# A state space scan of 62 steps, divided by groups between VectorE and GpSimd

## The reference, cut to what matters

```
state[c + 1] = a8 * state[c] + s[c + 1]        (complex, a8 = a to the power 8)
```

## Time and profile before

| | us |
|---|---|
| median of 3 runs | 3091.88 (3086.79 to 3098.38) |
| the profiled execution, its own time | 3087.09 |
| its span | 3084.8 |
| TensorE busy | 2834.6 (92%) |
| VectorE busy | 1872.8 (61%) |
| ScalarE busy | 1415.3 (46%) |
| GpSimd busy | 261.6 (8%) |

### The profile page before, as it was taken

How to read it: one execution, slowest core, us unless ns; L and a number is a source line. 1 busy time by engine, 2 the same in 40 slices (tenths; PEclk the granted TensorE clock), 3 DMA queues, 4 the chain that set the end, 5 groups by cost and what they waited for, 6 DMA issues and landing times.

```text
span 3084.8 us, 35846 instructions
## 1 busy us (share of the span) xinstructions
PE 2834.6 (92%) x12864; PEld 2221.4 (72%) x12864; DVE 1872.8 (61%) x2184; ACT 1415.3 (46%) x1806; POOL 261.6 (8%) x267
## 2 busy tenths in 40 slices
PE   7999999995999999999996469999989989899998
PEld 2547888874777777777775358888877767788887
DVE  3435654454889899898988684544333785354432
ACT  2323333323777777777775423333223347433321
POOL 1100100061001001010111000000011100000000
PEclk9999999995999999999998779999999999899999
DMA  6920722313898999999896612222221110022221
GB/s 237 334 85 30 284 111 96 125 55 150 342 372 350 380 357 368 367 358 375 349 376 223 57 67 82 96 96 96 96 91 69 55 55 28 28 96 96 96 96 69
DMA packets 90801, 546.93 MB, mean 177 GB/s; under 512 B 9232, under 2 KB 18848, under 8 KB 32384
## 3 DMA queue, kind: packets, MB, share of 16 engines
q1 hardware_dynamic: 79584, 485.65, 42.2%
q0 software_dynamic: 10816, 59.58, 5.5%
q10 hardware_dynamic: 288, 0.15, 0.0%
HBM read 516.51 MB, written 41.42 MB: 181 GB/s over the span
## 4 chain that ended last, share of the span: by engine, by line
PE 74%; DVE 14%; issue 6%; ACT 4%; DMA 1%; POOL 1%; DVEq 0%; ACTq 0%; SPq 0%; POOLq 0%; PEldq 0%
PE bank L400 41%; PE bank L338 6%; PE bank L1284 6%; PE bank L1288 5%; PE bank L1287 5%; DVE expert_low L2345 3%; ACT expert_high L1744 1%; PE bank L1268 1%; PE bank L1535 1%; DVE expert_x_low L2430 1%; DVE arena L2474 1%; PE bank L1469 1%; DVE arena L2561 1%; DVE arena L2560 1%; PE bank L1392 1%
## 5 line engine op out<-in xcount | busy, mean ns | idle before, releaser
L2345 DVE TENSOR_TENSOR expert_low<-arena,expert_high 128x2048 fp32r<-128x2048 f32 x291 | 690.2, 2403 | 89.5 <-ACT expert_high L1744 71.9
L1744 ACT ACTIVATE expert_high<-arena 128x1024 fp32r<-128x1024 f32 x582 | 599.3, 1059 | 203.4 <-PE bank L1284 120.4
L803 DVE TENSOR_TENSOR weight_parts<-ring_pages,weight_parts 128x1024 fp32r<-128x1024 f32 x185 | 227.0, 1227 | 458.3 <-ACT weight_parts L795 457.9
L795 ACT ACTIVATE weight_parts<-ring_pages 128x1024 fp32r<-128x1024 f32 x185 | 195.9, 1060 | 450.6 <-PE bank L400 407.1
L400 PE MATMUL bank<-high_b,weight_parts 128*128 128x512 f32 x1168 | 372.6, 401 | 13.0 <-DVE low_p L2583 7.4
L400 PE MATMUL bank<-low_b,weight_parts 128*128 128x512 f32 x1056 | 353.9, 389 | 0.0
L1284 PE MATMUL bank<-expert_high,expert_x_low 128*128 128x512 f32 x768 | 305.3, 398 | 23.5 <-DVE expert_low L2345 21.9
L1288 PE MATMUL bank<-expert_low,expert_x_high 128*128 128x512 f32 x768 | 300.4, 391 | 0.0
L1287 PE MATMUL bank<-expert_high,expert_x_high 128*128 128x512 f32 x768 | 300.1, 391 | 0.0
L400 PEld LDWEIGHTS bank<-high_b,weight_parts 128*128 128x128 f32 x1168 | 219.4, 190 | 75.6 <-issue 25.0
L400 PEld LDWEIGHTS bank<-low_b,weight_parts 128*128 128x128 f32 x1056 | 198.2, 188 | 41.6 <-issue 0.5
(11 more groups left out here) (479 smaller groups left out, 4407.8 us busy)
## 6 DMA issues: line engine op xcount, KB each, us to landing
arena<-in_we_stream SPq DMA_DIRECT2D x294, 1024.0 KB, 6.6
ring_pages<-in_wb_stream SPq DMA_DIRECT2D x93, 1024.0 KB, 4.8
ring_pages<-in_wa_stream SPq DMA_DIRECT2D x49, 1024.0 KB, 4.8
arena<-in_mod POOLq DMA_DIRECT2D x16, 1024.0 KB
xbuf<-arena POOLq DMA_DIRECT2D x25, 512.0 KB, 15.9
arena<-xbuf SPq DMA_DIRECT2D x17, 512.0 KB, 7.3
ybuf<-arena SPq DMA_DIRECT2D x16, 512.0 KB, 2.6
arena<-kd SPq DMA_DIRECT2D x8, 512.0 KB, 21.2
```

The source lines that it names most:

```text
L795: nc.scalar.activation(high, src, ACT.Copy).then_inc(weights_high, 1)
L803: nc.vector.tensor_tensor(low, src, high.bitcast(F32), ALU.subtract).then_inc(weights_split, 1)
L1744: nc.scalar.activation(ehigh[c % HIGH_E][:, at], ring_e[c % RING_E][:, at], ACT.Copy) \
L2345: nc.vector.tensor_tensor(elow[c % RING_E][:], ring_e[c % RING_E], ehigh[c % HIGH_E][:].bitcast(F32), ALU.subtract).then_inc(weights_split ...
```

## The change

VectorE keeps groups 0 to 43 and GpSimd gets groups 44 to 63, so that a VectorE instruction covers 128 x 88 elements and a GpSimd one 128 x 40. GpSimd's 62 steps have the same form as VectorE's. TensorE waits for a signal of both.

```diff
+SCAN_DVE = 44
...
@@ GpSimd's stream, behind the DMAs of kd @@
+            pool.wait_ge(S["b_s_copied"], KT)
+            pool.wait_ge(S["b_upper_copied"], 3 * KT)
+            rest = slice(SCAN_DVE, S5G)
+            for c in range(1, S5C - 1):
+                steps[0] += 2
+                nc.gpsimd.tensor_tensor(scaled[:, 0, :, rest], xs[:, c, :, rest], ab8[:, 0, :, rest], ALU.mult) \
+                    .then_inc(pool_step, 1)
+                nc.gpsimd.tensor_tensor(scaled[:, 1, :, rest], xs[:, c, ::-1, rest], ab8[:, 1, :, rest], ALU.mult) \
+                    .then_inc(pool_step, 1)
+                pool.wait_ge(pool_step, steps[0])
+                link(nc.gpsimd.tensor_tensor(xs[:, c + 1, :, rest], xs[:, c + 1, :, rest], scaled[:, 0, :, rest], ALU.add))
+                link(nc.gpsimd.tensor_tensor(xs[:, c + 1, :, rest], xs[:, c + 1, :, rest], scaled[:, 1, :, rest], ALU.add))
+            pool.sem_inc(S["b_scanned"], 1)
@@ TensorE's stream @@
-            pe.wait_ge(S["b_scanned"], 1)
+            pe.wait_ge(S["b_scanned"], 2)
@@ VectorE's stream @@
-            ts = scaled
+            first = slice(0, SCAN_DVE)
+            ts = scaled[:, :, :, first]
             for c in range(1, S5C - 1):
-                part(nc.vector.tensor_tensor(ts[:, 0], xs[:, c, :, :], ab8[:, 0], ALU.mult))
-                part(nc.vector.tensor_tensor(ts[:, 1], xs[:, c, ::-1, :], ab8[:, 1], ALU.mult))
+                part(nc.vector.tensor_tensor(ts[:, 0], xs[:, c, :, first], ab8[:, 0, :, first], ALU.mult))
+                part(nc.vector.tensor_tensor(ts[:, 1], xs[:, c, ::-1, first], ab8[:, 1, :, first], ALU.mult))
                 dve.wait_ge(dve_step, steps[0])
-                link(nc.vector.tensor_tensor(xs[:, c + 1], xs[:, c + 1], ts[:, 0], ALU.add))
-                link(nc.vector.tensor_tensor(xs[:, c + 1], xs[:, c + 1], ts[:, 1], ALU.add))
+                link(nc.vector.tensor_tensor(xs[:, c + 1, :, first], xs[:, c + 1, :, first], ts[:, 0], ALU.add))
+                link(nc.vector.tensor_tensor(xs[:, c + 1, :, first], xs[:, c + 1, :, first], ts[:, 1], ALU.add))
             dve.sem_inc(S["b_scanned"], 1)
```

## The result

| | before | after |
|---|---|---|
| median of 20 runs each, us | 3091.05 (3082.48 to 3103.69) | 3099.39 (3088.12 to 3102.23) |
| span of the profiled execution, us | 3084.8 | 3097.3 |
| GpSimd busy, us | 261.6 | 325.6 |
| VectorE busy, us | 1872.8 | 1878.8 |

The ratio of the times is 1.0018, with a 95% interval of 1.001 to 1.0027: slower by 5.6 us (3.1 to 8.3). The ratio isn't the quotient of the medians in the table, which are 8.3 us apart, at the upper end of that interval; the means are 6.3 us apart. This text goes by the ratio. The effect is less than 0.5%, and it is clear of zero with twenty runs of each, though the executions of one kernel lie up to 21 us apart. The forecast had the sign, and 12.5 us.

What follows compares the result with a forecast made beforehand. The prediction took VectorE's scan, with TensorE waiting behind it, as the bound here. GpSimd's own pace (7.5 us) plus waits between the engines (5 us) gave 3091.9 + 12.5 = 3104.4 us, range 3088 to 3128.

Steps and rivals of the forecast that it cites:

- The bound: VectorE's scan of 62 steps, 73.1 us, keeps TensorE waiting; each microsecond of its end counts one for the whole.
- VectorE's share: VectorE's scan instructions at 88 elements take 251 ns, a step 1.01 us, 62 steps 62.8 us instead of 73.1.
- GpSimd's share: GpSimd's undisturbed scan of 20 groups: 0.266 us an instruction, 1.30 us a step, 80.9 us, ending 7.5 us later than before.
- The price of one meeting: In the scan, each engine keeps the other out for its own instruction's duration less 0.14 us.
- The meetings: GpSimd's scan instructions meet VectorE in 43% of cases, waiting 0.055 us on average: 5 us; bounds nothing and 27 us.
- reading in turns: Lower bound of the waits in the scan: the engines fall into step and read in each other's gaps, costing nothing.
- Lockstep: Rival: nearly every scan instruction on both engines waits for most of the other's hold; end 27 to 35 us later; chance 0.29.
- whole instructions exclude each other: Rival: the engines' scan instructions never overlap, 2.07 us a step, end 55 us later, 3147 us; chance 0.07.
- GpSimd quicker than its rows: Rival: GpSimd's scan step is 0.91 to 1.06 us with overlapping products, end 5 to 10 us earlier; chance 0.09.
- The signs of being wrong: In the later profile: VectorE's last addition after GpSimd's, VectorE's mean above 0.29 us, GpSimd's tail off 1.30, or chain length changed.
- The sum: The scan ends 7.5 + 5 = 12.5 us later, so the whole takes 3104.4 us, 0.4% more.

Runs made afterwards that it cites:

- e2: The changed kernel with GpSimd's part of the scan left out, VectorE doing 44 groups alone: scan 63.3 us, ratio 0.9963 to the kernel before.
- e6: The kernel before, VectorE alone, with the first addition of a step waiting for the first product only: scan 65.9 us, ratio 0.9979.
- e1: The changed kernel with VectorE's part of the scan left out, GpSimd doing 20 groups alone: step 1.264 us, scan 78.5 us, one execution.
- e4: The changed kernel split into 60 groups on VectorE and 4 on GpSimd: step 1.188 us, scan 74.1 us, one execution.
- e8: The changed kernel with 52 and 12 groups and both products of a step in one instruction on both engines: scan 63.0 us, ratio 0.9955 to before.
- e5: The changed kernel with GpSimd's first product linked too, so its second waits for it: step 1.431 us on GpSimd, scan 88.9 us, one execution.
- e3: The changed kernel split into 52 groups on VectorE and 12 on GpSimd: step 1.157 us, scan 72.0 us, ratio 0.9993 to the kernel before.
- e7: The changed kernel with 52 and 12 groups and the first addition waiting for the first product only, on both engines: scan 66.0 us, ratio 0.9975 to before.
- e10: The changed kernel split into 40 groups on VectorE and 24 on GpSimd: step 1.341 us, scan 83.4 us, one execution.

## Why the prediction was right and wrong

**The bound: right.** The scan was on the path, TensorE had idle time to spare, and a microsecond of the scan was one of the whole but for 1.5 us (below). e2 shows it from the other side: 10.3 us less scan, 11 us less time. TensorE's work beside the scan even ran at half the clock for a while (0.52 from 1800 to 1810, below) and ended near 1820, still 18.1 us early. So the 25 us that a shorter scan could gain aren't a fixed sum: in e6, without GpSimd, TensorE's other work ended at 1816.8, only 3.5 us before the scan's end released it.

**VectorE's share: right to 2 ns** undisturbed (e2). That it doesn't set the end was right as well, but it didn't end at about 68 us, 10 ahead of GpSimd: it ended with it, 0.1 us later.

**GpSimd's share: the right engine, a third of the 7.5 us too much.** The instruction was right to 2 ns (0.266 forecast, 0.268), and so was the spacing behind a linked one (0.346 forecast and measured). The term that failed is the first product's spacing, which I took as 0.266 us from two long unlinked instructions; e1 has 0.225. This was a misreading of the row. 2.53 us for two is less than twice 1.29: they overlap. Each by itself in the kernel before:

```profile
2473.20 1.27 POOL L1061 TENSOR_TENSOR arena<-arena 128x512 f32<-128x512 f32 x1 [16.89 <-PE bank L1469]
...
2474.43 1.29 POOL L1061 TENSOR_TENSOR arena<-arena 128x512 f32<-128x512 f32 x1
```

The second starts 1.23 us behind the first, which lasts 1.27: 0.04 us of overlap. Taken from 0.266 that gives 0.226, within 1 ns of what e1 measured. It is 62 x 0.041 = 2.5 us of the 7.5 that GpSimd alone was to come later; e1 has 4.9 (78.5 against 73.6).

**The price of one meeting: right.** It was the duration less 0.14 us. For GpSimd's 0.267 that is 0.127; VectorE comes 0.063 behind, so it should wait 0.064, and waited 0.06. In e4 VectorE's second product (0.27 us) should shut GpSimd out for 0.13; line 1054 comes 0.016 behind it and waited 0.116. In e8 the product of 0.374 us should shut it out for 0.234; line 1051 comes 0.216 behind it and waited 0.017. What failed is how often the two meet, and who waits.

**The meetings: the term that was most out.** It was 5 us; e1 against the changed kernel gives 0.5. The step that failed is "a GpSimd instruction that comes at any time meets it in 43% of cases": the arrivals are not at any time. VectorE, the quicker engine, is held up until GpSimd's instruction lets it in, and so arrives again just behind GpSimd's next instruction. It takes all the waits (62 x 4 x 0.06 = 15 us, which it had to spare), and GpSimd's 248 instructions together are 0.4 us longer than in e1. I had named the lower bound, reading in turns, as the case in which the price is nothing; nothing in the rows of before told that two loops of the same form would end there. Meetings by chance are in no run: in e5, with the forms unlike, GpSimd paid 2.9 us, but in a rhythm that is fixed as well.

**The rivals.** Lockstep came, but not as I priced it: I had both engines pay at each meeting, 27 to 35 us. That whole instructions exclude each other for their full length would have been 55 us. By that rule (the Trainium skill, "SBUF — State Buffer", sections "SBUF: two separate sides" and "Who interferes with whom") VectorE, beginning 0.06 us behind a GpSimd instruction of 0.267, would wait 0.2 us; it waited 0.06. That one engine is kept out agrees (whether it is by the reads, no run here separates), that it lasts the whole instruction doesn't. GpSimd quicker than its rows: the unlinked pair did overlap, as that rival had it, but the linked spacings stayed at 0.35 us, which decided it.

**The signs of being wrong.** Three of those that the forecast named came. VectorE's last addition is later than GpSimd's, by 0.1 us, and its signal releases TensorE. VectorE's mean is 0.31 us, above 0.29, and GpSimd has no tail of its own. And the chain behind the scan is 1.5 us shorter, because TensorE's clock came back sooner (below); the forecast had moved that cost unchanged.

**The sum.** 7.5 + 5 = 12.5 forecast; 4.9 + 0.5 = 5.4 measured in the scan, and 5.6 by the ratio. The sign, a change below 0.5% and the range hold; the size was more than twice the truth. Of the 7.1 us too much in the scan, 4.5 are the meetings and 2.6 GpSimd's own share, almost all of it the spacing of the first product.

## What to carry to other kernels

In a chain of short dependent instructions the elements are the small part of the cost: here VectorE pays 0.16 us for an instruction and 1 ns for an element, GpSimd 0.18 us and 2.15 ns, and a wait for completion puts 0.04 (VectorE) or 0.08 us (GpSimd) between two instructions that would otherwise overlap: one wait fewer on VectorE (e6), or one more on GpSimd (e5), moved the step by 0.12 us (in e5 apart from the meetings). With four instructions a step the best split took 1.6 us from the scan, where one wait fewer took 7.7 and one instruction fewer 4.1; with three instructions a step the split took another 6.5. A second engine is worth adding only if its own undisturbed step is clearly shorter than the step of the first engine alone: 1.264 against 1.180 lost, 1.03 against 1.056 gained nothing, 0.99 (by estimate) against 1.113 gained 0.10. Where two loops of the same form kept step, the slower one paid next to nothing (0 to 0.04 us a step of 1.0 to 1.3): price the split by the slower engine alone, at its undisturbed pace.

## What the runs showed of the hardware that was not expected

- The two engines fall into a fixed rhythm, one to one in six kernels (after, e3, e4, e7, e8, e10) and four to three in e5. In four of these (after, e3, e7, e10) GpSimd is the slower and VectorE is stretched to fit, from 0.249 to 0.31 us at 88 elements and to 0.33 at 80.
- Two unlinked GpSimd instructions overlap by 0.04 us, at 40 elements (e1) and at 512 alike.
- How soon TensorE's clock comes back isn't fixed. It was at half for some 6 us after TensorE took up work at 1826.15 before; in the changed kernel, after 1838.46, some 3 us. The stages of the changed kernel (length, busy times, then the clock):

```profile
1800.00:1810.00 10.00, 10.00 (x30) 4.97 (x29) 9.20 (x32) 0.00 (x0) 8.18 (x32) 0.52 0.00 0
...
1838.00:1840.00 2.00, 1.54 (x7) 1.54 (x8) 0.31 (x1) 0.00 (x0) 0.24 (x1) 0.50 0.03 8
1840.00:1842.00 2.00, 2.00 (x15) 2.00 (x14) 0.44 (x1) 1.53 (x2) 0.00 (x0) 0.68 0.00 0
1842.00:1844.00 2.00, 2.00 (x21) 2.00 (x20) 1.92 (x2) 1.76 (x2) 0.00 (x0) 1.00 0.00 0
```

  The 64 matmuls that follow the scan took 10.23 us before and 8.7 after, which is the 1.5 us given back; over the traces of the study they took 8.7 to 10.2 us, with no order by the length of the scan.
